# Delta rule's inverse in sixteen array tiles for four heads and two blocks at once, later levels turned; compressed products in column groups

## The reference: three layers over 256 tokens

```python
def gated_deltanet(...):                      # q, k, v: eight heads, in chunks of c tokens
    gc = jnp.cumsum(chunks(gdec[..., None])[..., 0], axis=-1)
    decay = jnp.exp(jnp.where(lower_incl, gc[..., :, None] - gc[..., None, :], -jnp.inf))
    kb = k * beta[..., None]
    lmat = jnp.where(strict, jnp.einsum('bhnid,bhnjd->bhnij', kb, k) * decay, 0.0)
    tinv = lax.linalg.triangular_solve(eye + lmat, eye, left_side=True, lower=True)
    u = tinv @ (v * beta[..., None])
    w = tinv @ (kb * jnp.exp(gc)[..., None])
    attn = jnp.einsum('bhnid,bhnjd->bhnij', q, k) * decay
    def step(state, xs):
        v_new = u_i - w_i @ state
        o_i = q_i @ state + attn_i @ v_new
        state = state * jnp.exp(gl_i) + k_i.T @ v_new

def compress_blocks(t, pe, w1, w2):           # 15 blocks of 32 tokens, 16 apart
    blk = jnp.swapaxes(t[:, idx], 2, 3) + pe
    blk = blk.reshape(b, n_cmp, hk, CMP_BLOCK * d)
    return jax.nn.gelu(blk @ w1) @ w2
```

## Time and profile before

| | |
|---|---|
| median of 3 runs | 2351.98 us (2351.9 to 2352.14) |
| profiled execution | 2353.76 us |
| its span, first to last instruction | 2352.4 us |
| mean granted TensorE clock | 0.997 of full |
| TensorE busy | 2313.6 us (98%), 11190 matmul records |
| VectorE, ScalarE busy | 1368.8 us (58%), 1159.8 us (49%) |
| delta rule, first and second half | 884 to 977 us and 1034 to 1130 us |
| compressed products | 1157 to 1201 us |

### The profile page before, as it was taken

One profiled execution on the slowest core, in us unless ns is written; L12 is line 12 of the kernel. 1 busy time (PEld: TensorE's weight loads), 2 busy tenths in 40 slices (PEclk: granted clock), 3 DMA queues, 4 the chain that ended last, 5 costly groups with the idle time before them and its releaser, 6 DMA issues.

```text
span 2352.4 us, 27404 instructions
## 1 busy us (share of the span) xinstructions
PE 2313.6 (98%) x11190; PEld 1923.8 (82%) x11190; DVE 1368.8 (58%) x1937; ACT 1159.8 (49%) x1636; POOL 9.6 (0%) x17
## 2 busy tenths in 40 slices
PE   8999999999999999999999999999999999999998
PEld 6888788888788888888888887888888888888886
DVE  5776555656555667686666555655545544454554
ACT  5556654556654564453445455445444344434444
POOL 0000000000000000000000000000000000000000
PEclk9999999999999999999999999999999999999999
DMA  7454445554545543342554445555555555555553
GB/s 263 141 179 146 154 150 196 179 179 148 175 154 193 159 161 108 125 138 95 173 185 143 161 162 179 179 196 190 187 185 190 197 182 193 187 189 197 184 191 108
DMA packets 204557, 400.10 MB, mean 170 GB/s; under 512 B 12688, under 2 KB 12848, under 8 KB 204304
## 3 DMA queue, kind: packets, MB, share of 16 engines
q1 hardware_dynamic: 201920, 390.03, 49.1%
q0 software_dynamic: 1648, 6.32, 0.9%
q10 hardware_dynamic: 864, 2.00, 0.2%
HBM read 396.23 MB, written 2.10 MB: 169 GB/s over the span
## 4 chain that ended last, share of the span: by engine, by line
PE 92%; DVE 4%; ACT 2%; issue 1%; DMA 0%; ACTq 0%; SPq 0%; DVEq 0%
PE ACC L802 27%; PE ACC L804 27%; PE ACC L803 27%; PE TP L431 2%; ACT arena L825 1%; DVE WL L1700 1%; PE PV L633 1%; PE SC L628 1%; PE PV L636 1%; PE SC L468 1%; PE TP L476 1%; PE SC L679 1%; PE PV L485 0%; PE PV L486 0%; PE PV L484 0%
## 5 line engine op out<-in xcount | busy, mean ns | idle before, releaser
L1700 DVE TENSOR_TENSOR WL<-W,WH 128x1024 fp32r<-128x1024 f32 x740 | 901.2, 1220 | 651.5 <-ACT WH L825 649.6
L825 ACT ACTIVATE WH<-W 128x1024 fp32r<-128x1024 f32 x740 | 781.4, 1056 | 835.8 <-PE ACC L804 832.8
L802 PE MATMUL ACC<-WH,XH 128*128 128x512 f32 x2592 | 1046.9, 404 | 9.8 <-DVE WL L1700 4.0
L804 PE MATMUL ACC<-WH,XL 128*128 128x512 f32 x2592 | 1013.5, 391 | 0.0
L803 PE MATMUL ACC<-WL,XH 128*128 128x512 f32 x2592 | 1011.4, 390 | 0.0
L802 PEld LDWEIGHTS ACC<-WH,XH 128*128 128x128 f32 x2592 | 488.4, 188 | 115.0 <-issue 9.0
L804 PEld LDWEIGHTS ACC<-WH,XL 128*128 128x128 f32 x2592 | 487.2, 188 | 105.2
L803 PEld LDWEIGHTS ACC<-WL,XH 128*128 128x128 f32 x2592 | 488.9, 189 | 92.6 <-issue 1.0
L802 PE MATMUL ACC<-WH,HH 128*128 128x512 f32 x352 | 138.6, 394 | 0.0
L804 PE MATMUL ACC<-WH,HL 128*128 128x512 f32 x352 | 137.1, 389 | 0.0
L803 PE MATMUL ACC<-WL,HH 128*128 128x512 f32 x352 | 137.1, 389 | 0.0
(11 more groups left out here) (260 smaller groups left out, 1410.4 us busy)
## 6 DMA issues: line engine op xcount, KB each, us to landing
W<-in_w_in SPq DMA_DIRECT2D x84, 1024.0 KB, 4.8
W<-in_a_w_in SPq DMA_DIRECT2D x48, 1024.0 KB, 5.1
W<-in_w_ffn_gate SPq DMA_DIRECT2D x44, 1024.0 KB, 5.1
W<-in_w_ffn_up SPq DMA_DIRECT2D x44, 1024.0 KB, 5.1
W<-in_w_ffn_down SPq DMA_DIRECT2D x44, 1024.0 KB, 5.0
W<-in_b_w_in SPq DMA_DIRECT2D x40, 1024.0 KB, 5.0
W<-in_a_w_out SPq DMA_DIRECT2D x16, 1024.0 KB, 5.0
W<-in_b_w_out SPq DMA_DIRECT2D x16, 1024.0 KB, 5.0
```

Source lines behind the costliest of these rows:

```text
L802: MM(out, hx, WH[:, k, 0:ch.width], start=q == 0 and k == 0, stop=False)
L804: ins = MM(out, lx, WH[:, k, 0:ch.width], start=False, stop=last and k == QK - 1)
L825: return nc.scalar.activation(out, in_, func, **how)
L1700: TT(tiles_of(M.WL[n % 2], ch, half), tiles_of(M.W[n % 4], ch, half), tiles_of(M.WH[n % 2], ch, half).bitcast(F32), ALU.subtract).then_inc ...
```

## The change

- `dn(i)` replaces `dn(i, s)`: one generator for the four heads of a half, and both blocks t of 128 tokens go through the inverse together. The operations on VectorE and ScalarE become 512 columns wide. Each half has its own scratch.
- The first five levels, within diagonal blocks of 32, are done on the 32 x 32 blocks alone. ScalarE cuts them out of L (LB). VectorE masks them (MB), its own 32 x 32 transpose gives the first inverse. For each of the levels 1 to 4, TensorE transposes the blocks S (two full transposes) and does 32 matmuls of 32 x 32 by 32 columns (2 blocks t, 4 diagonal blocks b, 4 heads h), for which the start partition of operands and output picks one of sixteen array tiles; ScalarE copies both results out; 32 more such matmuls give the update, which VectorE subtracts.
- `widened` spreads the blocks back to 128 x 128. Levels 5 and 6 are done at full width, with the transpose TI made anew by TensorE (four transposes) in place of its own update.
- The state of the first block is read after the inverse (`dn_state_read`), in a step of its own.
- SC and PV become one tensor of four banks, so that one copy can read from all four.
- `compress(j)`: the blocks BL are the weights (padded to 32 columns) and W1 is the moving operand. Four column groups sum a quarter of the 32 products each, sixteen matmuls to a visit. One more matmul with `quarters` adds the four quarters; ScalarE copies in between.
- `compressed` and `nsa_attend` start two visits later.

```diff
-        begin(after("c.v0") + 11, "dn", 0, s)
-        begin(after("c.v1") + 32, "dn", 1, s)
+    begin(after("c.v0") + 11, "dn", 0)
+    begin(after("c.v1") + 32, "dn", 1)
...
-    begin(after("c.kv2") + 29, "compressed")
+    begin(after("c.kv2") + 31, "compressed")
...
-        begin(after("c.nq1") + 2 + 50 * g, "nsa_attend", g)
+        begin(after("c.nq1") + 4 + 50 * g, "nsa_attend", g)
...
+    M.banks = ctx.enter_context(nc.psum_tensor("SCPV", [P, 4, CH], F32))[:, :, :]
+    M.SC, M.PV = [M.banks[:, i, :] for i in range(2)], [M.banks[:, 2 + i, :] for i in range(2)]
```

TensorE's part:

```diff
+        def decays_and_keys(t):
+            pe.wait_ge(*at("dn_decay_steps", i, t))
+            wait_empty(f"SC{t}")
+            MM(SC[t][:, :], M.dn["ones"], flat(m["R"][t]), start=True, stop=True).then_inc(*did("dn_decay_rows", i, t))
+            wait_empty(f"PV{t}")
+            for h in range(HQ):
+                ins = MM(of(PV[t], h), block(1, h, t), block(1, h, t), start=True, stop=True)
+            ins.then_inc(*did("dn_keys_squared", i, t))
+        def query_keys(t):
+            for h in range(HQ):
+                ins = MM(of(TP[1], h), block(1, h, t), block(0, h, t), start=True, stop=True)
+            ins.then_inc(*did("dn_query_keys", i, t))
+        def decay_transposed(t):
+            pe.wait_ge(*at("dn_decayed", i, t))
+            pe.wait_ge(*at("dn_values_scaled", i, t))
+            for h in range(HQ):
+                ins = TR(of(TP[0], h), m["D"][t][:, h, :], ident)
+            ins.then_inc(*did("dn_decay_transposed", i, t))
+        def block_product(level):
+            pe.wait_ge(*at("dn_block_solved", i, level - 1))
+            for t in range(TB):
+                TR(of(banks[:, 0, :], 2 + t), flat(m["SB"][:, t]), ident)
+            for t, b, h in quarters:
+                ins = MM(banks[part(h), b, part(t)], m["MB"][part(b), t, h, :], m["SB"][part(b), t, h, :], start=True, stop=True)
+            ins.then_inc(*did("dn_block_product", i, level))
+        def block_update(level):
+            pe.wait_ge(*at("dn_block_taken", i, level))
+            for t, b, h in quarters:
+                ins = MM(banks[part(b), h, part(t)], m["TB"][part(h), t, b, :], m["PB"][part(h), t, b, :], start=True, stop=True)
+            ins.then_inc(*did("dn_block_update", i, level))
+        def level_product(t, level):
+            pe.wait_ge(*at("dn_solved", i, t, level - 1))
+            for h in range(HQ):
+                TR(of(TP[t], h), m["S"][t][:, h, :], ident)
+            for h in range(HQ):
+                ins = MM(of(SC[t], h), m["R"][t][:, h, :], m["S"][t][:, h, :], start=True, stop=True)
+            ins.then_inc(*did("dn_level_product", i, t, level))
+        def level_update(t, level):
+            pe.wait_ge(*at("dn_level_taken", i, t, level))
+            for h in range(HQ):
+                ins = MM(of(PV[t], h), m["TI"][t][:, h, :], m["Y"][t][:, h, :], start=True, stop=True)
+            ins.then_inc(*did("dn_level_update", i, t, level))
...
+        yield
+        for s in range(2):
+            pe.wait_ge(*at("dn_normed", i, s))
+            pe.wait_ge(*at("dn_activated", i, s, 2))
+            wait_empty(f"TP{s}")
+        for h in range(HQ):
+            TR(of(TP[0], h), block(1, h, 0), ident)
+            ins = TR(of(TP[1], h), block(2, h, 0), ident)
+        ins.then_inc(*did("dn_kv_transposed", i, 0))
+        decays_and_keys(0)
+        yield
+        pe.wait_ge(*at("dn_values_scaled", i, 0))
+        query_keys(0)
+        decays_and_keys(1)
+        yield
+        decay_transposed(0)
+        yield
+        pe.wait_ge(*at("dn_decay_taken", i, 0))
+        for h in range(HQ):
+            ins = TR(of(TP[0], h), block(2, h, 1), ident)
+        ins.then_inc(*did("dn_kv_transposed", i, 1))
+        yield
+        pe.wait_ge(*at("dn_scores_decayed", i, 0))
+        query_keys(1)
+        yield
+        block_product(1)
+        decay_transposed(1)
+        yield
+        for level in range(1, BLOCK_LEVELS):
+            block_update(level)
+            yield
+            if level + 1 < BLOCK_LEVELS:
+                block_product(level + 1)
+                yield
         for t in range(TB):
+            pe.wait_ge(*at("dn_scores_decayed", i, t))
+        level_product(0, BLOCK_LEVELS)
+        yield
+        for level in range(BLOCK_LEVELS, LEVELS):
+            level_update(0, level)
+            level_product(1, level)
+            yield
+            if level + 1 < LEVELS:
+                level_product(0, level + 1)
+            else:
+                pe.wait_ge(*at("dn_solved", i, 0, level))
+                new_sums(0)
+            level_update(1, level)
+            yield
...
+        pe.wait_ge(*at("dn_state", i))
+        for h in range(HQ):
+            ins = MM(of(SC[0], h), block(1, h, 1), m["STATE"][:, h, :], start=True, stop=True)
+        ins.then_inc(*did("dn_state_read", i))
+        yield
...
```

TensorE's compressed products:

```diff
         pe.wait_ge(*at("blocks_laid", j))
         for n in range(32):
-            ins = MM(SC[j][:, 0:2 * NC2], M.W1[:, n, :], M.BL[:, n, :], start=n == 0, stop=n == 31)
-            if n % 8 == 7:
+            rows = slice(PADC * (n % 4), PADC * (n % 4 + 1))
+            ins = MM(SC[j][rows, 0:HD], M.BL[:, n, :], M.W1[:, n, :], start=n < 4, stop=n >= 28)
+            if n % 16 == 15:
                 if n == 31:
                     ins.then_inc(*did("hidden_multiplied", j))
                 yield
-        emptied[f"SC{j}"] = ("hidden_activated", j)
+        emptied[f"SC{j}"] = ("hidden_taken", j)
+        yield
+        yield
+        wait_empty(f"TP{j}")
+        pe.wait_ge(*at("hidden_taken", j))
+        pe.wait_ge(*at("quarters_stacked"))
+        MM(TP[j][:, 0:2 * NC2], M.HT[j], M.quarters, start=True, stop=True).then_inc(*did("hidden_summed", j))
+        emptied[f"TP{j}"] = ("hidden_activated", j)
+        yield
```

ScalarE's and VectorE's parts (the copies and the order of VectorE's first steps):

```diff
+        def block_taken(level):
+            act.wait_ge(*at("dn_block_product", i, level))
+            A(m["TB"].rearrange("p t b w -> p (t b w)"), banks[:, 0, 2 * P:4 * P], ACT.Copy)
+            A(m["PB"].rearrange("p t b w -> p b t w"), banks[:, :, 0:TB * BK].rearrange("p b (t w) -> p b t w", t=TB), ACT.Copy).then_inc(*did("dn_block_taken", i, level))
+        def level_taken(t, level):
+            act.wait_ge(*at("dn_level_product", i, t, level))
+            A(flat(m["TI"][t]), TP[t][:, :], ACT.Copy)
+            A(flat(m["Y"][t]), SC[t][:, :], ACT.Copy).then_inc(*did("dn_level_taken", i, t, level))
...
+        decayed(0)
+        yield
+        act.wait_ge(*at("dn_decay_masked", i, 1))
+        A(flat(m["QD"]), SC[1][:, :], ACT.Exp)
+        decayed(1)
+        yield
+        decay_taken(0)
+            act.wait_ge(*at("dn_strict", i, t))
+            for b in range(4):
+                ins = A(m["LB"][part(b), t, :, :], m["L"][t][part(b), :, part(b)], ACT.Copy)
+        ins.then_inc(*did("dn_blocks_cut", i))
...
+        def decay_logs(t):
+            dve.wait_ge(*at("dn_decay_rows", i, t))
+            TT(m["D"][t], over_heads(M.dn["lower"]), heads(SC[t][:, :]), ALU.subtract).then_inc(*did("dn_decay_masked", i, t))
+            dve.wait_ge(*at("dn_decay_masked", i, t))
+            TT(m["D"][t], m["D"][t], per_head(of(GC, t)), ALU.add).then_inc(*did("dn_decay_logs", i, t))
+        def strict(t):
+            dve.wait_ge(*at("dn_decayed", i, t))
+            dve.wait_ge(*at("dn_keys_squared", i, t))
+            TT(m["L"][t], heads(PV[t][:, :]), m["D"][t], ALU.mult).then_inc(*did("dn_lower", i, t))
+            dve.wait_ge(*at("dn_lower", i, t))
+            TT(m["L"][t], m["L"][t], per_head(of(B, t)), ALU.mult).then_inc(*did("dn_strict", i, t))
+        def scores_decayed(t):
+            dve.wait_ge(*at("dn_decay_taken", i, t))
+            dve.wait_ge(*at("dn_query_keys", i, t))
+            TT(m["D"][t], heads(TP[1][:, :]), m["D"][t], ALU.mult).then_inc(*did("dn_scores_decayed", i, t))
...
+        decay_logs(0)
+        TT(m["KD"], heads(TP[0][:, :]), per_head(of(EKD, 0)), ALU.mult)
+        TT(m["VB"][0], heads(TP[1][:, :]), per_head(of(B, 0)), ALU.mult).then_inc(*did("dn_values_scaled", i, 0))
+        yield
+        decay_logs(1)
+        strict(0)
+        yield
+        strict(1)
+        TT(m["QD"], y[0][:, :, P:2 * P], m["QD"], ALU.mult)
+        yield
+        scores_decayed(0)
+        dve.wait_ge(*at("dn_blocks_cut", i))
+        block_masked(0).then_inc(*did("dn_first_blocks", i))
+        dve.wait_ge(*at("dn_first_blocks", i))
+        V.transpose(m["TB"].rearrange("p t b w -> p (t b w)"), m["MB"].rearrange("p t h w -> p (t h w)")).then_inc(*did("dn_first_turned", i))
+        dve.wait_ge(*at("dn_first_turned", i))
+        block_masked(1)
+        TT(flat(m["SB"]), over_blocks(masks[:, BLOCK_LEVELS, :]), flat(m["TB"]), ALU.subtract).then_inc(*did("dn_block_solved", i, 0))
+        yield
+        dve.wait_ge(*at("dn_kv_transposed", i, 1))
+        TT(m["VB"][1], heads(TP[0][:, :]), per_head(of(B, 1)), ALU.mult).then_inc(*did("dn_values_scaled", i, 1))
```

(75 more changed lines are left out.)

268 lines of the change are left out of this document (95 added, 173 removed).

## The result

The changed kernel takes 2318.72 us (median of 4 runs, 2317.59 to 2319.27) against 2352.06 us before: 33.3 us less, ratio 0.9849, 95% interval 0.9828 to 0.9871. The forecast was 2341.0 us, 11.0 us less. The direction was right and the size was three times too small.

The account below looks back on a forecast made before the run. TensorE, busy 98% of the span, was taken to bound the kernel; -42.7 + 31.7 + 3.7 + 3.0 - 7.1 + 0.4 = -11.0 us gave 2341.0 us. Own range 2334 to 2351; 8-in-10 range 2318 to 2367.

Parts of the forecast that it names:

- What bounds the kernel: Whole kernel: one long TensorE stream, busy 98% of the span; other engines count only where they make TensorE wait.
- Removed, 42.7 us: Delta rule on TensorE: 384 full-width records fewer at 0.1113 us each, 42.7 us less.
- Added small matmuls, 31.7 us: Block levels of the delta rule: 1024 records of 32x32 matmuls at 31 ns each, 31.7 us more.
- Rival (a): Block levels: small matmuls in different tiles overlap in full, 12 ns a record, 2322 us; chance 0.14.
- Rival (b), turns within a row group: Block levels: load and move of neighbouring small matmuls share a row group and take turns, 51 ns, 2362 us; chance 0.25.
- Rival (c), a fixed pace of 0.11 us: Block levels: a fixed pace of issue, not columns, sets each small record's price, 114 us in all, 2423 us; chance 0.07.
- Rival (d), the clock: Small streams count as idleness and the clock falls to 1.2 GHz, 2360 to 2380 us; chance 0.06.
- Mode changes, 0.23 us: Delta rule: entering and leaving the tiled mode costs 0.23 us a round trip, 3.7 us for sixteen streams.
- New waits, +3.0 us: Delta rule: TensorE waits longer for VectorE in the second and sixth visits, +3.0 us in two halves.
- Compressed products, -7.1 us: Compressed products: 128 records with 32-column weights at 40 ns, 5.1 us for 13.6, with mode changes and sums -7.1 us.
- L1586, +0.4 us: Ahead of the compressed products: clear and sum for the quarters delay the VectorE line TensorE waits for, +0.4 us.

Follow-up runs that it names:

- the first experiment: Changed kernel plus 32 more small matmuls ahead of each block product, over all sixteen tiles, one row group, one column group or one tile by level: 2329.47 us.
- the later starts: First compressed product started two visits later in the kernel before, the new delta rule alone and the changed kernel: 2348.75, 2323.18 and 2314.18 us.

## Why the prediction was right in sign and wrong in size

**What bounds the kernel: right.** TensorE's busy time fell by 39 us and the profiled span by 36.2. The 2318.72 us measured lie outside the forecast's own range of 2334 to 2351, and just inside the lower end of the wide one, 2318.

**Removed, 42.7 us: right.** The sixteen full-width groups of after sum to 392 records, as counted.

**Added small matmuls, 31.7 us: this step failed, and it is the miss.** It measured 10.6 ns a record and, with the mode changes, 14.3 us where 35.4 stood. I had reasoned that loads and moves of one array overlap with each other, and took the longer of the two for 32 columns as the floor. That is the price in one tile: 33 ns by the first experiment. Streams that change the tile with each matmul pay a third, because what runs in different tiles overlaps as well. Rival (a), 12 ns and 2322 us with a chance of 0.14, is what happened; I held against it that "the load of before is never faster than 0.86 ns a column", though no load that the earlier trace rows shows is one of several small ones side by side, so these rows could not speak against it.

The figure of the Trainium skill quoted under (a) (TensorE: Matmul & The Clock Gate, "Measured speedup vs the span model") is lower still: about 4 ns for each further tile. No whole stream here reaches it; the fastest cost 9 to 10 ns a record, with 32 or 8 moving columns.

**Rival (b), turns within a row group: wrong.** A stream over the four column groups of one row group goes as fast as one over all tiles (0.65 us both). I had also priced it for too many streams: only the product runs over four tiles of one row group, the update runs over four row groups. If the rival held, products would be slower than updates, and both take 0.68 us. The rule of the Trainium skill that I quoted (TensorE: Matmul & The Clock Gate, "The mechanism") has loads overlap only between row groups; the stream in one row group, 10 ns a record, does not agree for fp32, and the measurement decides. That loads overlap between row groups it does not contradict.

**Rival (c), a fixed pace of 0.11 us: wrong.** A small record with 8 moving columns costs 33 ns even in one tile, so L566's 0.105 us was no pace of issue; it fits the load of 128 columns.

**Rival (d), the clock: not in the kernel as it is.** The clock is 1.00 through the block levels. But it is real for a stream in one tile: behind three of the four added one-tile streams in the traces of the two runs it fell with no long wait ahead (behind the fourth it stayed at 1.00). The windows of the run with 8 columns show it, right behind its level 1 product.

```profile
902.00:903.00 1.00, 1.00 (x80) 0.98 (x77) 0.00 (x0) 0.00 (x0) 0.00 (x0) 1.00 0.74 84
...
904.00:905.00 1.00, 1.00 (x4) 0.81 (x3) 0.00 (x0) 1.00 (x2) 0.00 (x0) 0.50 1.04 406
```

**Mode changes, 0.23 us: right** for a stream that is entered and left once: an update costs 0.89 us with them and 0.68 without, 0.21. Inside a stream they cost 0.22 each where three are put in, and 0.02 where one is.

**New waits, +3.0 us: too high.** L611, L638 and L618 wait 2.7 us where L628 had 1.8, so +0.9; with one break of 1.0 us inside a small stream, which I had not foreseen, +1.9. The two places named (second visit for the scaled values, sixth for the first scores) are the two L611 rows, 0.5 and 0.4 us each time where I had 1.0 and 1.3; the widened blocks I had not seen.

**Compressed products, -7.1 us: right in mechanism, 2 us short.** They measured 9.2 by the landmarks and 9.0 with the later starts. A stream costs (1159.29 - 1157.62) less 0.45 = 1.2 us with its mode changes where I had 1.5; over four streams that is 1.1 us. A full-width stream of before is 1.79 us with the pause behind it, not 1.70; over eight streams that is 0.7 us, and most of the gap is closed. Half clock has no part in it: it is 3.4 us long in both traces, and the 9.0 us hold without it.

**L1586, +0.4 us: about right.** The wait for the blocks grew by 0.2, and the compressed start by the landmarks by 0.4.

The sum with measured terms: -42.7 + 14.3 + 1.9 - 9.2 + 0.4 = -35.3 us. The profiled spans differ by 36.2, of which 1.6 lie ahead of the change, which leaves 34.6, and the medians by 33.3.

## What to carry to other kernels

Where a stream of small matmuls is costed, ask whether its neighbours lie in different tiles, not how long one load takes: four tiles in turn gave a third of the price of one tile, and each stream pays 0.2 us to enter and leave the tiled mode. Two matmuls in a row in one tile are nearly harmless, four in a row double the price. And look at what TensorE waits for just ahead of a window with half clock: a wait of 2 us cost 3 to 12 us here, and two visits of delay removed it.

## What the hardware showed that I had not expected

- Behind the same wait of 2.0 to 2.3 us, half clock lasted 3.4 us in the traces of five runs (before and after among them), was missing in three (both runs with added matmuls, and the new compressed products alone), and lasted over 20 us in the new delta rule with the old compressed products, there by the mean clock in three of four executions. The kernel before had three executions of 33 at 2360 to 2362 us, two of them with a listed mean clock of 0.993 and 0.994; their traces are not kept. What decides the length stays open; without the wait it was gone in all four.
- Small streams break at times, mostly for 0.6 to 1.1 us, with nothing to wait for ("issue"): once in the changed kernel (1.0 us), five times in the run with 64 more records in each product (2.7 us in all, the shortest of them 0.2). No run here shows the cause. One guess is untested: the page's DMA queue of the kind "instruction" brings 16 KB every 24 us between the two halves of the delta rule but every 3 to 9 us in the block levels, so instructions may come late there.
- A small fp32 record in one tile costs 33 ns with 32 or with 8 moving columns.
- A stream of 64 records over all tiles is not even in itself. In the trace of the changed kernel the first 32 records start within 0.15 us, 4.9 ns apart; then stands a gap of 0.09 us, and the other 32 take 0.32 us. All but two of the sixteen streams show it alike. No run says why.
